# VectorE forms u_lo in the experts stage of a two-layer diffusion step, and GpSimd only issues the gathers

## The reference, cut to what matters

```python
def peer_layer(h, w_q, subkeys, u_tab, v_tab):
    ...
        g = jax.nn.softmax(sc.astype(jnp.float32), axis=-1).astype(xt.dtype)
        act = jax.nn.gelu(jnp.einsum('thkd,td->thk', jnp.take(u_tab, eidx, axis=0), xt))
        return jnp.einsum('thk,thkd->td', g * act, jnp.take(v_tab, eidx, axis=0))
```

## Time and profile before

| what | value |
|---|---|
| median of 3 runs | 4360.15 us (4359.65 to 4360.77) |
| the profiled execution, its own time | 4353.85 us |
| its span, first to last instruction | 4351.9 us |
| mean granted TensorE clock over the span | 0.943 |
| experts stage, starts of `v_lo` from first to last block | 1042.8 to 2195.9 us and 3156.9 to 4311.3 us |

### The profile page before, as it was taken

The page is one execution under the profiler, slowest core; times in us unless marked ns, Lnnn a source line. Parts: engine busy times, 40 slices in busy tenths (PEclk is TensorE's granted clock), DMA queues, the critical chain, the costliest instruction groups (busy, mean ns, idle before and its releaser), DMA issues. The chain is left out here.

```text
span 4351.9 us, 60760 instructions
## 1 busy us (share of the span) xinstructions
PE 3904.6 (90%) x20790; PEld 3246.6 (75%) x20790; DVE 3500.1 (80%) x6404; ACT 1409.8 (32%) x2566; POOL 2560.7 (59%) x1810
## 2 busy tenths in 40 slices
PE   8879989978999999999969989897899999999996
PEld 1876789367888878888858758863688887888885
DVE  0234658988999999999950456699899999999998
ACT  1331232165333233333333122314733323333332
POOL 0300023588888888888822001228888888888884
PEclk9876989989999999999979599998999999999998
DMA  6311011547999999999931000144599999999996
GB/s 257 109 42 41 1 41 59 213 175 293 357 355 359 358 359 371 379 373 378 376 112 66 8 39 21 60 156 175 213 359 360 356 357 356 363 377 376 377 379 224
DMA packets 300883, 1047.86 MB, mean 241 GB/s; under 512 B 30032, under 2 KB 82000, under 8 KB 290480
## 3 DMA queue, kind: packets, MB, share of 16 engines
q0 software_dynamic: 147456, 536.94, 32.3%
q1 hardware_dynamic: 153264, 508.85, 31.8%
HBM read 992.11 MB, written 53.56 MB: 240 GB/s over the span
## 5 line engine op out<-in xcount | busy, mean ns | idle before, releaser
L1807 DVE CUSTOM_DVE_ANT_0 picked_rows<-picked_rows,h2rows 128x1024 f32<-128x1024 f32 x512 | 939.7, 1852 | 0.0
L1815 DVE SCALAR_TENSOR_TENSOR y<-picked_rows,dots_now,y 128x1024 f32<-128x1024 f32 x512 | 872.3, 1723 | 0.0
L1703 PE MATMUL ps<-hd_hi,u_hi 128*128 128x384 f32 x2048 | 723.1, 353 | 142.6 <-POOL u_lo L1772 110.9
L1530 POOL DMA_INDIRECT picked_rows<-in_u_rows,chosen x512 | 737.9, 1441 | 164.2 <-issue 133.4
L1530 POOL DMA_INDIRECT picked_rows<-in_v_rows,chosen x512 | 592.8, 1158 | 200.4 <-DVE y L1815 109.1
L1703 PE MATMUL ps<-hd_hi,u_lo 128*128 128x384 f32 x2048 | 696.0, 340 | 0.0
L1703 PE MATMUL ps<-hd_lo,u_hi 128*128 128x384 f32 x2048 | 695.6, 340 | 0.0
L1772 POOL TENSOR_TENSOR u_lo<-u_raw,u_hi 128x1024 fp32r<-128x1024 f32 x256 | 650.4, 2541 | 25.6 <-ACT u_hi L1737 21.0
L1752 ACT ACTIVATE a_hi<-ps 128x384 fp32r<-128x384 f32 x256 | 126.0, 492 | 1443.9 <-DVE ps L1793 1443.9
L1703 PEld LDWEIGHTS ps<-hd_hi,u_hi 128*128 128x128 f32 x2048 | 386.2, 189 | 246.1 <-POOL u_lo L1772 168.5
L1714 PE MATMUL ps<-v_hi,a_hi 128*128 128x512 f32 x1536 | 479.5, 393 | 8.5 <-DVE v_lo L1801 8.5
(11 more groups left out here) (304 smaller groups left out, 7368.7 us busy)
## 6 DMA issues: line engine op xcount, KB each, us to landing
u_raw<-in_u SPq DMA_DIRECT2D x256, 512.0 KB, 9.2
v_raw<-in_v SPq DMA_DIRECT2D x256, 512.0 KB, 7.2
gates_dram<-gmat SPq DMA_DIRECT2D x12, 4096.0 KB, 11.5
gt<-gates_dram SPq DMA_DIRECT2D x64, 768.0 KB, 11.8
wq<-in_ada_w SPq DMA_DIRECT2D x16, 2048.0 KB, 7.9
wring<-in_ada_w SPq DMA_DIRECT2D x12, 2048.0 KB, 8.0
w_raw<-in_w_in SPq DMA_DIRECT2D x18, 1024.0 KB, 4.8
wq<-in_wq SPq DMA_DIRECT2D x8, 2048.0 KB, 8.0
```

The costliest lines, as they stand in the source:

```text
L1530: pool.indirect_dma_start(picked_rows[:, n % RING, :], None, a[table], bass.IndirectOffsetOnAxis(ap=chosen[:, m % GT, m // GT:m // GT + 1] ...
L1703: ins = pe.matmul(ps[:, b % 2, 0:TD], (u_hi, u_lo)[wl][:, b % 2, k, :], (hd_hi, hd_lo)[hl][:, k, :], start=(k == 0 and n == 0), stop=(k == ...
L1807: dve.tensor_tensor_reduce(row, row, h2rows[:, m % GT, :], 1.0, 0.0, ALU.mult, ALU.add, dots_now[:, m % GT, m // GT:m // GT + 1]).then_inc ...
L1815: dve.scalar_tensor_tensor(to, row, dots_now[:, m % GT, m // GT:m // GT + 1], to, ALU.mult, ALU.add).then_inc(row_used, 1)
```

## The change

`u_lo` moves from GpSimd to VectorE. The subtraction itself is the same: same operands, shape, types and semaphores. On VectorE, `low_u(b + 2)` stands in block b between the first gathered row and `low_a(b)`; `low_u` of blocks 0 and 1 stands ahead of the clearing of `y`. GpSimd's program in this stage now holds gathers alone. The last body of VectorE is written out once more outside the loop, because its last two blocks have no `low_u`.

```diff
             @block.gpsimd
             def _(pool):
-                def low_u(j):
-                    pool.wait_ge(u_high, j + 1)
-                    pool.tensor_tensor(u_lo[:, j % 2, :, :], u_raw[:, j % 4, :, :], u_hi[:, j % 2, :, :],
-                                       ALU.subtract).then_inc(u_split, 1)
-
-                low_u(0)
-                low_u(1)
                 for j in range(NKEYS):
-                    if j + 2 < NKEYS:
-                        low_u(j + 2)
                     for n in range(RING + PER * j, min(RING + PER * (j + 1), 2 * DOTS)):
                         pool.wait_ge(row_used, n - RING + 1)
                         gather(pool, n)
...
             @block.vector
             def _(dve):
                 link = chain_of(dve, f_chain)
+
+                def low_u(g, b):
+                    dve.wait_ge(u_high, g * BODY + b + 1)
+                    dve.tensor_tensor(u_lo[:, b % 2, :, :], u_raw[:, b % 4, :, :], u_hi[:, b % 2, :, :],
+                                      ALU.subtract).then_inc(u_split, 1)
+
+                low_u(0, 0)
+                low_u(0, 1)
                 link(dve.memset(y[:, :, :], 0.0))
...
-                def body(g, picked_row):
+                def body(g, picked_row, last=False):
                     for b in range(BODY):
                         gate(g, b)
                         picked_row(g, PER * b)
+                        if not last or b < BODY - 2:
+                            low_u(g, b + 2)
                         low_a(g, b)
                         picked_row(g, PER * b + 1)
                         picked_row(g, PER * b + 2)
...
-                with dve.Fori(0, BODIES - DOT_BODIES) as i:
+
+                def weights(i):
                     dve.wait_ge(row_used, i * (BODY * PER) + DOTS)
                     dve.tensor_copy(dots_now[:, :, :], dots[:, :, bass.ds(i * each, each)]).then_inc(weights_now, 1)
                     dve.wait_ge(weights_now, i + 1)
+
+                with dve.Fori(0, BODIES - DOT_BODIES - 1) as i:
+                    weights(i)
                     body(i + DOT_BODIES, weigh)
+                weights(BODIES - DOT_BODIES - 1)
+                body(BODIES - 1, weigh, last=True)
```

## The result

The changed kernel takes 4159.8 us (median of 4 runs, 4159.27 to 4159.96) against 4359.9 us before (4358.34 to 4360.77). The ratio is 0.9541, 95% interval 0.9525 to 0.9558: faster by 200 us, where 144 were forecast.

What follows compares the result with a forecast made beforehand. VectorE, frozen by GpSimd's subtraction, was taken as the bound. Gains of 114 + 28 + 0 + 2 = 144 us took 4353.85 to 4210; adding 6.3 gave 4216 us, range 4165 to 4250 (elsewhere 4290).

Steps and rivals of the forecast that it cites:

- part 4: TensorE is late next in the experts stage: `hidden` 4.34 us plus `outputs` 4.13 us, 8.47 us per block.
- allowance: Some waiting among VectorE, TensorE and transfers, raising 8.47 us to 8.50 per dot block and 8.60 per weigh block.
- dot half: First half of each layer's experts stage: blocks fall from 9.39 to 8.50 us, 114 us gained over two layers.
- weigh half: Second half of each layer's experts stage: blocks fall from 8.83 to 8.60 us, 28 us gained over two layers.
- last two blocks: End of each layer's experts stage: no `u_lo` there either way, so 0 us gained.
- entry: Start of each layer's experts stage: first `u_lo` takes 1.21 instead of 2.41 us, 2 us gained in all.
- fast end: TensorE at 8.33 us per block in both halves of the experts stage, so 4161 us.
- parts 1 and 2: VectorE loses GpSimd's freeze (2.71 us per dot block, 1.68 per weigh block) and gains one subtraction (1.14 or 1.20 us).
- Part 5: Transfers move 3.34 MB per block: 8.15 us at 410 GB/s, 8.89 at 376; called the most doubtful term.
- Part 3: `low_u(b+2)` on VectorE waits for ScalarE's `u_hi`: taken as 0, with 0.49 us per block as the other end.
- Rival C: VectorE pays a 2.1 us wait before `u_lo` in every block: slower, about 4617 us, chance 0.05.
- Rival B: VectorE's two-input instructions lock out GpSimd's gathers, 1.98 us each: 4358 us, chance 0.07 shared with the 358 GB/s limit.

Runs made afterwards that it cites:

- pool_reads: Changed kernel plus one unread GpSimd subtraction of two 128x1024 f32 SBUF tensors per block: 4595.63 us, ratio 1.0556 to the kernel before.
- half_u: Kernel before, with GpSimd forming only half of each `u_lo` and `hidden` using that half for all eight slices: 4154.76 us, ratio 0.9543.
- transfers: Changed kernel without the third pass of `outputs` and with no `u_lo` formed (`hidden` reads `u_hi` instead): 4128.24 us, ratio 0.9464.
- pool_fills: Changed kernel plus one GpSimd fill of a spare 128x2048 f32 tensor per block, which reads nothing: 4203.87 us, ratio 0.9636.
- pool_copies: Changed kernel plus one GpSimd copy of 128x1024 f32 from SBUF to SBUF per block: 4276.31 us, ratio 0.9822.
- before_two: Kernel before without the third pass of `outputs`, 36 instead of 42 matmuls a block: 4345.04 us, ratio 0.9982.
- two_passes: Changed kernel without the third pass of `outputs`, 36 instead of 42 matmuls a block: 4131.4 us, ratio 0.949.

## Why the prediction was wrong

The mechanism held: the freeze went, VectorE fell below TensorE, TensorE became the bound at a granted clock of 1.00. What failed is the size of TensorE's block in the sum: 8.47 us in part 4 and an allowance on top, 8.50 and 8.60 in all, where the runs show 8.36. That is 18 and 29 us of the 56 by which the forecast missed. The terms, measured from the starts of `v_lo`, both layers:

| term | forecast | measured |
|---|---|---|
| dot half, 64 blocks | 114 us | 140 us |
| weigh half, 61 blocks | 28 us | 61 us |
| last two blocks | 0 | −4 us |
| entry | +2 us | −3.5 us |
| sum | 144 us | 194 us |

The 194 us are the difference of the two profiled executions (4351.9 to 4157.9). The other 6 us are in how the sum became a time. The prediction added 6.3 us, because the median before was that much above the profiled execution, and the changed kernel's median is level with its own (4159.8 and 4159.9). The kernel before has medians of 4353.78 and 4353.98 in some runs and of 4359.9 and 4360.47 in others; the changed kernel was timed only beside the latter two. Why the two levels, and whether the changed kernel has a lower one too, stays open. Without the 6.3 us the forecast would have been 4210 and the worked-out fast end 4155, below the measured time.

- **What bounds the kernel; parts 1 and 2: right, but for the weigh block.** VectorE's dot block without the freeze was worked out at 7.79 us. The blocks at the start of the stage, in which it runs ahead, are 7.78 apart (`v_lo` of blocks 0 and 1 starts at 1045.45 and 1053.23). The weigh block was worked out at 8.16 and takes 7.98: its 6.96 without the freeze should have been the 6.85 of the last blocks, and its 1.20 is 1.14. `pool_reads` and `half_u` show the cause.
- **Part 4 failed in one term.** It took `hidden` from its start to that of `outputs` in one block, 4.34 us. That block's first matmul takes 0.45 us where all others take 0.34, because it starts behind a wait. The next matmul starts 0.28 us behind it in place of 0.18. With the wait gone that extra 0.1 us goes too, `hidden` takes 4.24, and the block 8.36 in place of 8.47. The prediction had the better figure, 8.33 from the pace inside the run, and used it only as the far end.
- **The allowance failed.** On top of 8.47 the sum put 0.03 and 0.13 us, because three limits lay "within 4% of each other in the weigh half", "so some waiting among them is to be expected". There was none: TensorE was busy 200.00 of 200 us. VectorE was not that near either, at 8.05 us with the pauses in place of 8.35. With two to four buffers between engines, the limits did not add up here. 8.36 in place of 8.50 and 8.60 makes 47 of the 59 us by which the two halves came out better. The other 12 are `v_lo` getting further ahead of TensorE; most of it comes back in the rows for the entry and the last two blocks.
- **Part 5, the transfers: the doubt was unfounded by a hair.** 395 GB/s was needed, 400 to 405 was reached. The prediction read 376 GB/s at a DMA share of 0.99 as near the ceiling and put 22% on that. Transfers that only followed VectorE's demand looked just as busy. The 410 GB/s over 5 us was the better guide: `transfers` reaches 405 over 200 us. The Trainium skill, page "SBUF — State Buffer", section "SBUF: two separate sides", gives about 358 GB/s between HBM and a core. The trace does not agree: the changed kernel moved 400 and 405 GB/s over 200 us.
- **Part 3, the new wait, held:** ScalarE's waits for `u_raw` fell from 124.7 to 27.6 us in all, and VectorE waited 15.1 us for `u_hi` in the whole execution. Rival C had no ground.
- **The entry term had the wrong sign.** It counted the shorter first `u_lo` and not the load of the gates behind it, with `u_lo(2)` now in the queue after it: 2 × 1.14 = 2.3 us of the 3.5. The rest is when the first gates landed (the first gate product starts at 1038.39 before and at 1039.94 after). The last two blocks were taken as unchanged; VectorE now has to wait for TensorE there as well (15.76 us for 13.80).
- **Rival B** did not come about, yet its rule held. A VectorE instruction with two SBUF inputs does make a gather wait. Of the 1008 gathers in the experts stages of the changed kernel, all 642 of over 1.1 us end 0.8 to 0.9 us after such an instruction does, and the 29 that start under none take 0.94 at most. The median gather from u rose from 1.21 to 1.68 us. GpSimd had room for that, 152.60 of 200 us busy, and `pool_fills` shows how little room beyond.

The range ended at 4165 on the low side, though its own fast end was worked out at 4161, with TensorE at 8.33 us a block. It was rounded the wrong way, and the chance put on that end was too small. (With 4161 as its end it would still have missed the time by 1 us. Its high end stands as 4250 in one sentence and as 4290 in another.)

## What to carry to other kernels

When one instruction of a kind takes three times its median, look at what the other engine that shares its SBUF access runs over it. Here the instruction cost nothing on its own engine and 1.7 to 2.7 us on the neighbour, and one that takes 1.2 us on the neighbour was the better buy. To find the next bound, take the pace from inside an unbroken run of that engine's instructions, without the first one after a wait, and add nothing for other limits that are merely near when there are two or more blocks of buffer between them (one case, this one, bears that out). Judge the transfers by the highest rate held over some microseconds, not by the average at a high busy share.

## What the runs showed of the hardware that was not expected

- A GpSimd copy with one SBUF input holds up a VectorE instruction with two (2.05 us for 1.22), and a fill without any does not (1.33 us at most over 256 fills of 1.83). Instructions with an operand in PSUM pass (117 of them under a running GpSimd subtraction before, 0.57 us at most).
- The blocked VectorE instruction runs nearly its full length after GpSimd ends: all 250 held dots and weighs before end 1.08 to 1.10 us later, and the held ones in `pool_reads` and `pool_copies` 1.07 to 1.10.
- Starting first did not always help. A dot that had started 0.42 us before GpSimd's subtraction was held all the same, so that the overlap cost more (2.71 us) than the subtraction lasted (2.39). From 0.70 us on it passed, and the next one was held.
- Transfers of which six in ten bytes were 4 KB rows gathered by GpSimd's indirect transfers held 400 to 405 GB/s over stretches of 200 us on one core. The DMA share hardly tells such a stretch (1.02 and 1.03) from one at 376 GB/s (0.99).
- TensorE's granted clock stayed at 1.00 with the engine busy 200 of 200 us. In stretches of 200 us where it had pauses of 10 to 18% the mean granted clock was 0.95 to 0.98 in `before_two` and `transfers`, but 0.99 and 1.00 in `two_passes`, with pauses of 12 to 13%. What decides between them is not shown.
